# Turning the right half of the first normalised input by DMA in 16-bit planes, and a rearranged start

## The reference, cut to what matters

```python
def rmsnorm(x, g):
    y = x * lax.rsqrt(jnp.mean(x * x, axis=-1, keepdims=True) + EPS)
    return y * g

def swiglu(h, wg, wu, wd):
    return (jax.nn.silu(h @ wg) * (h @ wu)) @ wd

x = x + 0.5 * swiglu(rmsnorm(x, g_ffn1), w1_gate, w1_up, w1_down)   # 2048 -> 5632 -> 2048
...  # latent attention, dilated attention, gates, output projection, a second swiglu, a last gated projection
```

## Time and profile before

| | |
|---|---|
| median of 3 runs | 2352.56 us (2352.56 to 2352.81) |
| profiled execution, its time | 2351.54 us |
| its span in the trace | 2349.7 us |
| PE busy | 2342.6 us, 100% |
| DVE busy | 1911.8 us, 81% |
| ACT busy | 1521.1 us, 65% |
| POOL busy | 43.7 us, 2% |
| DMA queue of SP | 69.7% of 16 engines |

### The profile page before, as it was taken

One profiled execution on the slowest core, in us unless ns is written; L12 is line 12 of the kernel. 1 busy time (PEld: TensorE's weight loads), 2 busy tenths in 40 slices (PEclk: granted clock), 3 DMA queues, 4 the chain that ended last, 5 costly groups with the idle time before them and its releaser, 6 DMA issues.

```text
span 2349.7 us, 28124 instructions
## 1 busy us (share of the span) xinstructions
PE 2342.6 (100%) x10566; PEld 1943.7 (83%) x10566; DVE 1911.8 (81%) x2325; ACT 1521.1 (65%) x1821; POOL 43.7 (2%) x49
## 2 busy tenths in 40 slices
PE   9999999999999999999999999999999999999999
PEld 8888888888888888888888888888888888888887
DVE  6898889798887766767666778888989988897878
ACT  6666666764567765666676566576666666754665
POOL 0000000000000000000021000010000000000010
PEclk9999999999999999999999999999999999999999
DMA  7776767766577654877786777686676778666775
GB/s 249 208 231 201 219 206 217 225 201 213 183 229 200 200 167 140 222 223 206 217 202 162 215 214 208 196 242 205 197 232 203 216 218 230 200 206 196 225 211 179
DMA packets 319364, 488.54 MB, mean 208 GB/s; under 512 B 138424, under 2 KB 140416, under 8 KB 319232
## 3 DMA queue, kind: packets, MB, share of 16 engines
q1 hardware_dynamic: 318784, 486.47, 69.7%
q10 hardware_dynamic: 448, 0.34, 0.1%
HBM read 453.70 MB, written 2.10 MB: 194 GB/s over the span
## 4 chain that ended last, share of the span: by engine, by line
PE 98%; DVE 1%; ACT 0%; issue 0%; DMA 0%; POOL 0%; POOLq 0%; ACTq 0%
PE ps L696 38%; PE ps L718 12%; PE ps L720 12%; PE ps L719 12%; PE ps L845 7%; PE ps L847 7%; PE ps L846 7%; PE ps L1104 1%; PE ps L1092 1%; PE ps L914 0%; DVE wl L1853 0%; ACT wh L1244 0%; PE ps L1225 0%; DMA raw<-in_w_o 0%; DVE res L2048 0%
## 5 line engine op out<-in xcount | busy, mean ns | idle before, releaser
L1853 DVE TENSOR_TENSOR wl<-raw,wh 128x1024 fp32r<-128x1024 f32 x764 | 925.2, 1225 | 352.3 <-ACT wh L1244 347.4
L1244 ACT ACTIVATE wh<-raw 128x1024 fp32r<-128x1024 f32 x763 | 796.6, 1054 | 511.6 <-PE ps L696 226.8
L718 PE MATMUL ps<-wh,hT 128*128 128x512 f32 x1156 | 451.7, 391 | 0.8 <-DVE vd L2155 0.5
L720 PE MATMUL ps<-wh,hT 128*128 128x512 f32 x1156 | 450.0, 389 | 0.0
L719 PE MATMUL ps<-wl,hT 128*128 128x512 f32 x1156 | 449.9, 389 | 0.0
L696 PE MATMUL ps<-wh,hT 128*128 128x512 f32 (+1 forms) x1456 | 392.3, 387 | 0.3 <-DVE vd L2155 0.3
L696 PEld LDWEIGHTS ps<-wh,hT 128*128 128x128 f32 x1456 | 269.1, 188 | 53.7 <-DVE vd L2155 0.5
L718 PEld LDWEIGHTS ps<-wh,hT 128*128 128x128 f32 x1156 | 217.1, 188 | 46.1 <-DVE vd L2155 0.9
L720 PEld LDWEIGHTS ps<-wh,hT 128*128 128x128 f32 x1156 | 217.0, 188 | 45.3
L719 PEld LDWEIGHTS ps<-wl,hT 128*128 128x128 f32 x1156 | 217.1, 188 | 44.7
L696 PE MATMUL ps<-wl,hT 128*128 128x512 f32 x728 | 222.0, 386 | 0.0
(11 more groups left out here) (449 smaller groups left out, 3376.1 us busy)
## 6 DMA issues: line engine op xcount, KB each, us to landing
raw<-in_w_in SPq DMA_DIRECT2D x208, 512.0 KB, 4.1
raw<-in_w_up SPq DMA_DIRECT2D x176, 512.0 KB, 4.6
raw<-in_w_down SPq DMA_DIRECT2D x176, 512.0 KB, 4.5
raw<-in_w_gate SPq DMA_DIRECT2D x175, 512.0 KB, 4.0
raw<-in_w_o SPq DMA_DIRECT2D x32, 512.0 KB, 4.7
raw<-in_w_ple_gate SPq DMA_DIRECT2D x32, 512.0 KB, 4.4
raw<-in_w_br_mla SPq DMA_DIRECT2D x16, 512.0 KB, 4.1
raw<-in_w_br_dil SPq DMA_DIRECT2D x16, 512.0 KB, 5.0
```

Source lines behind the costliest of these rows:

```text
L718: pe.matmul(ps[:, b0 + t, :], xh, wh[:, s, c], start=first, stop=False)
L720: mm = pe.matmul(ps[:, b0 + t, :], xl, wh[:, s, c], start=False, stop=last)
L1244: act.activation(wh[:, j % SLOTS, :], raw[:, j % SLOTS, :], ACT.Copy).then_inc(hi_ready, 1)
L1853: dve.tensor_tensor(wl[:, j % SLOTS, :], raw[:, j % SLOTS, :], wh[:, j % SLOTS, :].bitcast(F32), ALU.subtract).then_inc(lo_ready, 1)
```

## The change

The left half of x (quarters 0 and 1) is turned by TensorE as before; the right half, pairs 4 to 7, now goes through planes. Quarter 2 + q (q = 0, 1) is taken apart by GpSimd (low halves) and ScalarE (high halves), SP issues two transposes of 128x1024 16-bit values, GpSimd and ScalarE copy the planes together into `hQ`, and ScalarE (`x_high`) and VectorE (`x_rest`) make `hTh` and `hTl` from it. On ScalarE the taking apart stands at steps 3 and 5, the putting together at 5 and 8, the high parts at 6 and 9. On SP the transposes stand ahead of everything else at v = 10 and v = 12. At the start the gain row is fetched and transposed before pair 0, the two blocks of pair 0 have a semaphore each, two matmuls on `ones` replace three after pair 0, VectorE rounds the first half of the first weight, and unit 1 begins with the matmuls that do not need `wl` (`second_unit`).

```diff
@@ scalar: queue at the start
-            act.dma_start(ident[:, :], identity).then_inc(ident_in, 16)
             act.dma_start(grow_1[:, :], g_ffn1[0].rearrange("(k p) -> k p", p=P)).then_inc(row1_in, 16)
+            act.dma_start(ident[:, :], identity).then_inc(ident_in, 16)
@@ what TensorE turns before units 3, 7 and 10
-        X_TURNS = ((3, 1, 1, (2, 3)), (7, 6, 2, (4, 5)), (10, 9, 3, (6, 7)))
+        X_TURNS = ((3, 1, 1, (2, 3)),)
@@ sync
+            def turn_x(q):
+                sp.wait_ge(xq_lo, T * (2 * q + 1))
+                sp.wait_ge(xq_hi, T * (q + 1))
+                for t in range(T):
+                    sp.dma_start_transpose(planes_xT[q][t][:, :, :, :].rearrange("p b k s -> p (b k) s"),
+                                           planes_x[q][t][:, :, :].rearrange("p b c -> p (b c)")).then_inc(xq_in[q], 16)
             def gate_up(u0, w_gate, w_up, f):
                 for m in range(FFN_TURNS):
                     for v in range(FFN_BODY):
+                        if f == 0 and m == 0 and v in (10, 12):
+                            turn_x((10, 12).index(v))
@@ gpsimd
+            for q in range(2):
+                c0 = UNIT + q * BANK
+                pool.wait_ge(x_in[2 + q], 16)
+                for t in range(T):
+                    pool.tensor_copy(planes_x[q][t][:, 0, :], res_16[:, t, c0:c0 + BANK, 0]).then_inc(xq_lo, 1)
+                pool.wait_ge(xq_in[q], 16 * T)
+                for t in range(T):
+                    pool.tensor_copy(hQ_16[:, 4 * q:4 * q + 4, 1, t * P:(t + 1) * P, 0], planes_xT[q][t][:, 0, :, :])\
+                        .then_inc(xq_lo, 1)
@@ tensor: unit 1
+            def second_unit():
+                pe.wait_ge(hi_ready, 2)
+                for w, sides in ((wh, (hTh, hTl)), (wl, (hTh,))):
+                    if w is wl:
+                        pe.wait_ge(lo_ready, 2)
...
@@ tensor: the start
-            pe.wait_ge(x_first, 16)
-            turn(res, LEFT[0:1], 0)
             pe.wait_ge(row1_in, 16)
             pe.transpose(ps[:, 2, 0:KD], grow_1[:, :], ident[0:KD, 0:KD]).then_inc(gains_turned, 1)
-            for _ in range(WARM // 2):
+            pe.wait_ge(x_first, 16)
+            for s, done in ((0, first_turned), (1, turned)):
+                for t in range(T):
+                    mm = pe.transpose(ps[:, s, t * P:(t + 1) * P], res[:, t, s * P:(s + 1) * P], ident[:, :])
+                mm.then_inc(done, 1)
+            for _ in range(WARM // 3):
@@ scalar: entry(0, j)
+                    if j in (3, 5):
+                        x_apart((3, 5).index(j))
+                    if j in (5, 8):
+                        x_together((5, 8).index(j))
+                    if j in (6, 9):
+                        x_high((6, 9).index(j))
@@ scalar, vector: the first weight's first half
-            act.wait_ge(raw_first, 16)
-            act.activation(wh[:, 0, 0:BANK], raw[:, 0, 0:BANK], ACT.Copy).then_inc(first_hi, 1)
+            dve.wait_ge(raw_first, 16)
+            dve.tensor_copy(wh[:, 0, 0:BANK], raw[:, 0, 0:BANK]).then_inc(first_hi, 1)
@@ vector: entry(0, j)
+                    if j in (6, 9):
+                        x_rest((6, 9).index(j))
```

More of the change, by code:

```diff
@@ L236, in hybrid_layer @@
         planes_qT = [at(f"planes_qT{t}", (56 + 4 * t) * KB, [P, 2, KD // 2, P], U16) for t in range(T)]
+        planes_x, planes_xT = ([[at(f"{n}{q}{t}", (where + 8 * q + 2 * t) * KB, shape, U16) for t in range(T)] for q in range(2)]
+                               for n, where, shape in (("planes_x", 48, [P, 2, BANK]), ("planes_xT", 52, [P, 2, 4, P])))
         hQ = whole("hQ", 32 * KB, [P, KD // 2, 2, S])
@@ L248, in hybrid_layer @@
         hi_ready, lo_ready = sem("hi_ready"), sem("lo_ready")
-        unit_done, first_hi = sem("unit_done"), sem("first_hi")
+        unit_done, first_hi, first_turned = sem("unit_done"), sem("first_hi"), sem("first_turned")
         raw_first, x_first, x_in = sem("raw_first"), sem("x_first"), [sem(f"x_in{j}") for j in range(4)]
@@ L259, in hybrid_layer @@
         right_in = [sem(f"right_in{t}") for t in range(T)]
+        xq_lo, xq_hi = sem("xq_lo"), sem("xq_hi")
+        xq_in = [sem(f"xq_in{q}") for q in range(2)]
         sig_ready, am_ready, a_raw, ah_ready, a_ready = (
@@ L418, in turned_by_pe @@
         def turned_by_pe(pairs):
-            return pairs - sum(min(max(pairs - PAIRS[r], 0), KD // 2) for r in range(1, 4))
+            return pairs - min(max(pairs - KD // 4, 0), KD // 4) - sum(min(max(pairs - PAIRS[r], 0), KD // 2) for r in range(1, 4))
         block = ctx.enter_context(nc.Block())
@@ L782, in first_turn @@
                         pe.wait_ge(tr_lo, 2 * p + 2)
-                        square_unit(u0 + v, v, 2 * p, hTh, hTl, 4 + 2 * (v % 2), KD)
+                        if v == 1:
+                            second_unit()
+                        else:
+                            square_unit(u0 + v, v, 2 * p, hTh, hTl, 4 + 2 * (v % 2), KD)
                 pe.wait_ge(gcol_ready, 2)
+            def second_unit():
[4 more added lines that the diff above has]
+                    for t in range(T):
+                        for k in range(2):
+                            for a in sides:
+                                mm = pe.matmul(ps[:, 6 + t, :], a[:, k, t * P:(t + 1) * P], w[:, 1, k * BANK:(k + 1) * BANK],
+                                               start=(k == 0 and w is wh and a is hTh), stop=False)
+                mm.then_inc(unit_done, 1)
             def gate_up(u0, f):
@@ L1277, in squares, with x_apart, x_together, x_high @@
                                    accum_out=ssq[:, c:c + 1]).then_inc(ss_ready, 1)
+            def x_apart(q):
+                c0 = UNIT + q * BANK
+                act.wait_ge(x_in[2 + q], 16)
+                for t in range(T):
+                    act.activation(planes_x[q][t][:, 1, :], res_16[:, t, c0:c0 + BANK, 1], ACT.Copy).then_inc(xq_hi, 1)
+            def x_together(q):
+                act.wait_ge(xq_in[q], 16 * T)
+                for t in range(T):
+                    act.activation(hQ_16[:, 4 * q:4 * q + 4, 1, t * P:(t + 1) * P, 1], planes_xT[q][t][:, 1, :, :], ACT.Copy)\
+                       .then_inc(xq_hi, 1)
+            def x_high(q):
+                act.wait_ge(xq_lo, T * (2 * q + 2))
+                act.wait_ge(xq_hi, T * (q + 3))
+                for k in range(KD // 2 + 4 * q, KD // 2 + 4 * q + 4):
+                    act.activation(hTh[:, k, :], hQ[:, k - KD // 2, 1, :], ACT.Copy, scale=gcol[:, k:k + 1]).then_inc(tr_hi, 1)
             def right_apart(r):
@@ L1539, in _ @@
             act.wait_ge(gcol_ready, 1)
-            high(hTh, 0, 0, (0,), 0)
+            for s, done in ((0, first_turned), (1, turned)):
+                act.wait_ge(done, 1)
+                act.activation(hTh[:, s, :], ps[:, s, 0:S], ACT.Copy, scale=gcol[:, s:s + 1]).then_inc(tr_hi, 1)
             act.wait_ge(raw_in[0], 16)
@@ L1877, in _, with x_rest @@
             LEFT, RIGHT = range(KD // 4), range(KD // 4, KD // 2)
+            def x_rest(q):
+                for k in range(KD // 2 + 4 * q, KD // 2 + 4 * q + 4):
+                    dve.wait_ge(tr_hi, k + 1)
+                    dve.scalar_tensor_tensor(out=hTl[:, k, :], in0=hQ[:, k - KD // 2, 1, :], scalar=gcol[:, k:k + 1],
+                                             in1=hTh[:, k, :].bitcast(F32), op0=ALU.mult, op1=ALU.subtract).then_inc(tr_lo, 1)
             def right_rest(r, j):
@@ L2195, in attention @@
                 between(len(items) - 1)
-            rest(hTl, hTh, 0, 0, (0,), 0)
+            dve.wait_ge(raw_first, 16)
+            dve.tensor_copy(wh[:, 0, 0:BANK], raw[:, 0, 0:BANK]).then_inc(first_hi, 1)
+            for k in range(2):
+                dve.wait_ge(tr_hi, k + 1)
+                dve.scalar_tensor_tensor(out=hTl[:, k, :], in0=ps[:, k, 0:S], scalar=gcol[:, k:k + 1],
+                                         in1=hTh[:, k, :].bitcast(F32), op0=ALU.mult, op1=ALU.subtract).then_inc(tr_lo, 1)
+            dve.wait_ge(first_hi, 1)
             split(0, 0)
```

2 lines of the change are left out of this document (1 added, 1 removed).

## The result

The changed kernel takes 2355.72 us (median of 22 runs, 2354.2 to 2356.86), the kernel before, run beside it, 2351.98 us (22 runs, 2350.68 to 2353.56): a ratio of 1.0016, 95% interval 1.0010 to 1.0022. It is slower by 3.7 us. The forecast was 2359.3 us with a range of 2355.8 to 2362.0. The sign was right, and the size was not: the time lies 0.1 us under the range, and at 0.16% it falls within the 0.2% to which the prediction gave 0.18, not into the 0.80 for slower by more. The profiled execution took 2356.37 us, with a span of 2354.6 against 2349.7.

What follows compares the result with a forecast made beforehand. TensorE, busy 100%, was taken as the bound. Wait 6.4 plus clock 2.2, less transposes 1.75 and start 0.1, gave +6.7 us: 2358.3 profiled, with 1.02 to the median 2359.3 against 2352.56; range 2355.8 to 2362.0.

Steps and rivals of the forecast that it cites:

- Steps 1 to 8: Chain through ScalarE, SP and VectorE from quarter 2 to unit 8: blocks ready at 36.7, TensorE idle 6.4 us.
- step 1: ScalarE takes quarter 2 apart behind unit 7's split, which waits for TensorE to finish unit 3; done at 20.76.
- step 3: SP issues the first two transposes of 128x1024, holding it 4.15 us, until 26.15.
- step 5: Unit 10's weights land 4.5 us after the request, at 33.45; its split waits for them and ends at 34.5.
- the quick SP: Rival: SP issues transposes and gains faster, unit 10 asked for at 25.9, TensorE stands 2.4 us; +0.5 us, chance 0.10.
- the last rival: Worse case: first pair 5.68, landing 5.4, perhaps another wait before unit 12; +9.7 us, 2362.3, chance 0.08.
- The clock: TensorE's clock falls to half rate during the wait before unit 8, costing 2.2 us more, bounds 0 and 2.75.
- The first rival: The wait before unit 8 comes, but the clock stays up or is back at once: +4.75 us, 2357.3, chance 0.14.
- The start: Changes before unit 1 save 0.1 us, bounds 0 and 0.3.
- late by some 0.2: Second pair of transposes: blocks 12 and 13 ready about 47.8, unit 12 due at 47.6, if the clock stays up.
- The local sum: Delay from all terms: wait 6.4 plus clock 2.2, less transposes 1.75 and 0.1 at the start, +6.7 us.
- whatever moves there moves the end by the same amount: TensorE runs without a gap after the start, so an early delay or saving reaches the end in full.

Runs made afterwards that it cites:

- The first experiment: The changed kernel with the seven gain loads on SP ahead of the transposes: 2352.71 us against 2351.52 for the kernel before, ratio 1.0004.
- the tenth and eleventh: The change reordered, twice: planes taken apart and high parts made earlier, gains behind unit 11's weights, second transposes ahead of unit 14's; 2349.5 and 2349.3 us, ratios 0.9992 and 0.9989.
- the three profiles of the change: The changed kernel, its first run and two unedited repeats: 2355.72, 2356.0 and 2355.87 us; ratios to the kernel before 1.0016, 1.0017 and 1.0016.
- the ninth: The changed kernel with high parts and rests of blocks 8 to 11 moved ahead of unit 10's split: 2354.08 us, ratio 1.0012 to the kernel before.
- experiment 13: The kernel before with TensorE waiting idle ahead of eight units for 20 GpSimd memsets each: 2414.14 us, ratio 1.0269.
- experiment 12: The kernel before with 24 extra unused matmuls on ones ahead of each of eight units: 2394.49 us, ratio 1.0182.
- experiments 2 and 3: Against the kernel before: only the change's start, 2350.71 us, ratio 0.9997; then the change without its start (right half through planes), 2357.16 us, ratio 1.0022.
- The two kernels kept busy: The changed kernel with 20 or 24 unused matmuls (fillers) on TensorE ahead of unit 8: 2354.43 and 2355.35 us, ratios 1.0011 and 1.0014 to the kernel before.

## Why the prediction was right in kind and wrong in size

**The chain.** Steps 1 to 8 stand as written, and nearly all with the releaser that they name (at step 1 this profile puts the last 0.28 us ahead of the split of unit 7 down to its load, at the time that the forecast had for TensorE). Forecast and measured: SP starts 22.0 and 21.96, the pair 4.15 and 3.97, the gains 2.79 and 2.82, the load asked for at 28.95 and 28.79, landing in 4.5 and 3.93, the split of unit 10 at 33.45 and 32.74, unit 8 at 36.7 and 35.90. The first experiment undid the gains' part of it, the tenth and eleventh all of it, and the time followed both times.

**The size of the wait** is the first term that was off. It was put at 6.4 us; the three profiles of the change have an idle time of 5.35, 4.77 and 4.43. In the first, unit 8 was 4.56 later, not 5.4, and step 3 (0.18 too long) and step 5 (0.57) are nearly all of the difference. Step 5 took the middle of the landings of the earlier trace rows, 4.5, and the load of unit 10 landed in 3.9 in every profile of the change. Step 3 took 4.15 for the pair because it would be the first one, and it was 3.97, 3.38 and 3.07. In the ten profiles that have this path the first pair took 2.72 to 4.37 us, in six of them less than the 3.50 that the prediction had as the shortest. Even so the quick SP did not come: unit 10 was asked for at 28.8, 28.1 and 28.4, not before 25.4. Nor did the long pair of the last rival (5.68).

**The clock.** It fell, as forecast; the term was 2.2 and the spacing gives 2.24, 2.05 and 1.72 in the three profiles. The eight stands show that this is really paid. The first rival (the clock stays up) falls. So does one statement in the rival with a quick SP, that 2.4 us of standing are too short for the clock to fall: it fell in the stand of 2.35 us of the first experiment, which cost 1.6 us more, though not in the 2.87 us ahead of unit 12 in the ninth. That rival, counted with 0.5 us, would have read +2.1. The Trainium skill, in TensorE: Matmul & The Clock Gate, Part 1, has the array's clock halve after idleness and return after sustained work. The traces agree: it fell in all eight idle stands of experiment 13 and in none of the eight filled ones of experiment 12, where it stayed at 1.00.

**What was saved.** The two groups of transposes are gone, at 0.88 and 0.87. The start was put at 0.1 with an upper bound of 0.3; it is 0.0 in the profile, and the medians of experiments 2 and 3 read 0.8 and 1.2, within their noise. No further wait came at unit 12, and the ninth experiment shows that only the first stand hid it, by 2.9 us: "late by some 0.2" was too mild a view of a chain that gets no shorter when the first one does.

**The steps that failed.** The first is the stand, "TensorE stands still for 6.4 us": 0.9 to 1.8 us too long (TensorE's matmuls are 5.5, 4.9 and 4.6 us apart beyond their usual 0.227), from the pair of step 3 and the landing of step 5. The local sum was 6.7, and the three profiles give 5.98, 5.1 and 5.0. The second is the last step, from one profiled execution to the median: "would be 2358.3; the median of the runs is 1.02 above it". With 22 runs the profiled execution of before lies 0.44 under its median, not 1.02, so the forecast began 0.6 us too high.

The forecast was 3.6 us above the measured median. 0.6 is that offset. Of the other 3.0, 1.9 show in the traces: the spans of the three profiles are 4.9, 4.5 and 5.0 above that of before, 4.8 in the mean, where 6.7 was forecast. About 1.3 of the 1.9 is the local sum, and 0.6 is gone between 63 us and the end. The last 1.1 I put down to scatter between executions: the spans are 4.8 apart and the medians 3.7, since the profiled execution of before was a quick one (0.44 under its median) and those of the change were not (0.65, 0.0 and 0.7 above theirs).

What is gone by the end was put at nothing by "whatever moves there moves the end by the same amount". It is 1.1, 0.6 and 0.0 us in the three profiles. The kernel before has small waits of TensorE of its own in its profile (0.33 us at 267.6, 0.24 at 1532.4), and another execution need not meet them, delayed or not: the start alone, which is level with before near 63 us (+0.03), is 0.4 us under it at the end. So a part of the 1.1 has nothing to do with the delay. The rest was not tried.

**What stays open.** The two kernels kept busy are only 0.5 to 1.0 us under the change in the median, where 1.7 to 2.2 was to be expected. In the one with 24 fillers these held unit 8 by 0.5 us themselves. Each of these ratios has an interval of some 2 us to either side (0.0009 of 2352), and unit 8's begin moves by 0.7 between executions, so the two don't contradict the eight stands. They couldn't settle the question, and the eight stands did. Whether the start is worth the 0.8 to 1.2 us of its medians stays open too; if it is, it is a part of the 1.1 us that is put down to scatter here.

## What to carry to other kernels

A transpose by DMA costs the issuing queue as well as the transfer (here a pair held SP for 2.6 to 4.4 us): look first at which load that TensorE needs soon stands behind it, and put loads that have time (the gains here) on whichever side of it costs nothing. When a helper path replaces work of the engine that bounds the kernel, the saving is the small, certain part; what decides is where its pieces stand in the in-order streams. The same pieces in another order went from 3.7 us slower to 2.6 to 2.8 us faster. And when a term is 0.2% of the time, don't add the offset of a single execution to it; repeat the disputed cost several times in one program instead.

## What the runs showed of the hardware that was not expected

The granted clock can fall under running matmuls. In the third profile of the change it fell 0.8 us after the stand had ended, 5.3 us after the last matmul ahead of it. In the first profile of the change it fell 3.1 us after that matmul, in the first experiment 1.9. The half-rate stretch came in two lengths: 3.4 us in the first experiment and the third profile of the change, 6.8 us in the first two profiles of the change, in experiment 3 and in experiment 13. Why the one or the other comes is not shown.

In experiment 13 eight stands that are alike to 0.01 us (5.34 each) cost 2.8 and 1.75 us in strict turn. Stretches of its first and its second stand, in which the last filler ended at 96.28 and at 146.36:

```profile
100.00:101.00 1.00, 0.00 (x0) 0.00 (x0) 1.00 (x2) 0.92 (x3) 0.82 (x4) 0.82 0.00 0
...
107.00:108.00 1.00, 1.00 (x5) 0.81 (x4) 0.00 (x0) 0.79 (x1) 0.00 (x0) 0.77 0.00 0
```

```profile
148.00:148.50 0.50, 0.00 (x0) 0.93 0.00 0
...
155.00:155.50 0.50, 0.50 (x3) 0.75 1.09 422
```

(In the second fence TensorE alone was asked for, so its columns are busy time, granted clock, DMA share and GB/s.) A mean clock of 0.82 over the first microsecond puts the fall at 100.6, 4.4 us after the last filler, and the mean of 0.77 the return at 107.5. In the second stand they are 148.4, 2.1 us after it, and 155.25. Both half-rate stretches are 6.8 us long; the early one simply lies more within the stand, where it costs nothing. The same stand has two prices, then, and the one read from a single profile is one draw of them.
